# Two weight remainders of each state-space round on GpSimd, and the group's preparation done a round earlier

## The reference

```
h += 1/2 SwiGLU(RMSNorm(h))
u  = RMSNorm(h)
h += W_out( sum_b sigmoid(gate_b(u)) * P_b(mixer_b(u)) )   # linear attention, state space (SSD), chunk attention
h += 1/2 SwiGLU(RMSNorm(h));  out = RMSNorm(h)

SSD, for each of 8 groups (4 heads of 64, state 128), chunks of 64 tokens:
  x, B, C = silu(conv4(u @ w));  dt = softplus(..);  cum = cumsum(dt * a)
  y  = sum_s (C_t . B_s) * exp(cum_t - cum_s) * dt_s x_s        (s <= t, inside the chunk: "intra")
     + (C_t . state) * exp(cum_t)                                (from earlier chunks: "inter")
  state = exp(cum_last) * state + sum_s B_s (dt_s x_s exp(cum_last - cum_s))
  y  = RMSNorm_group((y + D x) * silu(z))
```

## Time and profile before

| | us |
|---|---|
| median of 3 runs | 1847.29 (1846.7 to 1848.17) |
| profiled execution | 1847.36 |
| its span, first to last instruction | 1845.5 |
| TensorE busy | 1806.9 |
| VectorE busy | 977.6 |
| ScalarE busy | 610.7 |
| GpSimd busy | 145.1 |

### The profile page before, as it was taken

How to read it: one execution, slowest core, us unless ns; L and a number is a source line. 1 busy time by engine, 2 the same in 40 slices (tenths; PEclk the granted TensorE clock), 3 DMA queues, 4 the chain that set the end, 5 groups by cost and what they waited for, 6 DMA issues and landing times.

```text
span 1845.5 us, 26225 instructions
## 1 busy us (share of the span) xinstructions
PE 1806.9 (98%) x9852; PEld 1508.4 (82%) x9852; DVE 977.6 (53%) x1376; ACT 610.7 (33%) x942; POOL 145.1 (8%) x116
## 2 busy tenths in 40 slices
PE   7999999999999999999999999999999999999997
PEld 5888888878888888788988888887888888888885
DVE  6444443379888888732444445545334544444333
ACT  4323222233333344332233334443222422323221
POOL 4111100031111111100000000000000011111000
PEclk9999999999999999999999999999999999999998
DMA  4323223322222222132222222222222322223331
GB/s 154 103 93 100 93 101 103 110 84 70 73 74 69 68 68 68 58 103 91 92 69 82 90 87 82 84 78 89 95 99 91 103 92 92 101 92 101 103 105 66
DMA packets 47352, 164.91 MB, mean 89 GB/s; under 512 B 5520, under 2 KB 6672, under 8 KB 47296
## 3 DMA queue, kind: packets, MB, share of 16 engines
q1 hardware_dynamic: 43584, 158.10, 26.1%
q10 hardware_dynamic: 3712, 6.03, 1.0%
HBM read 162.01 MB, written 2.10 MB: 89 GB/s over the span
## 4 chain that ended last, share of the span: by engine, by line
PE 70%; issue 21%; DVE 6%; POOL 1%; ACT 1%; DMA 0%; DVEq 0%; POOLq 0%; ACTq 0%; SPq 0%
PE G L534 33%; PE G L576 12%; PE I L534 9%; PE G L550 7%; DVE WL L1443 2%; DVE CV L1626 1%; PE I L896 1%; POOL hid L456 1%; PE I L930 1%; PE I L906 1%; PE I L704 1%; PE I L712 1%; PE G L761 1%; DVE UL L1459 1%; DVE un L1581 1%
## 5 line engine op out<-in xcount | busy, mean ns | idle before, releaser
L1443 DVE TENSOR_TENSOR WL<-RAW,WH 128x1024 fp32r<-128x1024 f32 x297 | 387.9, 1309 | 298.2 <-ACT WH L1025 290.2
L1025 ACT CAST WH<-RAW 128x1024 fp32r<-128x1024 f32 x297 | 309.6, 1048 | 230.9 <-PE I L534 126.2
L534 PE MATMUL G<-UH,WH 128*128 128x512 f32 x696 | 172.8, 390 | 0.0
L534 PE MATMUL G<-UH,WL 128*128 128x512 f32 x696 | 171.9, 389 | 0.0
L534 PE MATMUL G<-UL,WH 128*128 128x512 f32 x696 | 171.9, 389 | 0.0
L534 PEld LDWEIGHTS G<-UH,WH 128*128 128x128 f32 x696 | 130.6, 188 | 28.0 <-issue 1.0
L534 PEld LDWEIGHTS G<-UH,WL 128*128 128x128 f32 x696 | 130.6, 188 | 27.1
L534 PEld LDWEIGHTS G<-UL,WH 128*128 128x128 f32 x696 | 130.6, 188 | 27.1
L534 PE MATMUL G<-NH,WH 128*128 128x512 f32 x448 | 113.2, 395 | 1.4 <-ACT SC L1098 1.4
L534 PE MATMUL G<-NL,WH 128*128 128x512 f32 x448 | 110.7, 389 | 0.0
L534 PE MATMUL G<-NH,WL 128*128 128x512 f32 x448 | 110.6, 389 | 0.0
(11 more groups left out here) (299 smaller groups left out, 2477.5 us busy)
## 6 DMA issues: line engine op xcount, KB each, us to landing
RAW<-in_slabs SPq DMA_DIRECT2D x297, 512.0 KB, 3.3
h<-in_x SPq DMA_DIRECT2D x4, 512.0 KB, 6.8
bias<-in_rel ACTq DMA_DIRECT2D x16, 128.0 KB, 3.0
out_y<-h ACTq DMA_DIRECT2D x8, 256.0 KB, 2.2
bias<-in_rel ACTq DMA_DIRECT2D x16, 112.0 KB, 2.6
cst<-in_cst SPq DMA_DIRECT2D x1, 168.0 KB, 3.6
ut<-in_wgk SPq DMA_DIRECT2D x3, 32.0 KB, 8.8
```

The lines of the kernel that those rows point to most:

```text
L534: ins = mm(dst, W[:, n.slot, (k - k0) * P:(k - k0 + 1) * P], R[:, k, :], start=begin and which == 0 and k == k0, stop=end and which == 2 a ...
L1025: nc.scalar.copy(WH[:, n.slot, :], RAW[:, n.slot, :]).then_inc(split_hi, 1)
L1443: V.tensor_tensor(WL[:, n.slot, :], RAW[:, n.slot, :], WH[:, n.slot, :].bitcast(F32), ALU.subtract).then_inc(split_lo, 1)
```

## The change

GpSimd takes over the remainders of slabs n+5 and n+6 of each looped round (`lo`), and VectorE waits for them ahead of n+7 so that the count split_lo stays in order. GpSimd makes MSL of the next group in this round, and VectorE makes MSH (`da_hi`) behind the silu of CT, both from SC and no longer from gsc. D times x is made by ScalarE while it copies x (four pieces, one for each head), XTE and XDT are read from PSUM, XTE first, and TensorE's updates wait for both. The squares are scaled by 1/16 and come ahead of the tanh of t=3; the variance is an addition on GpSimd; ScalarE scales two of the four tiles of Y and VectorE the others. `ssm_y` comes after the silu of t=2. In `ssm_intra` the two halves of a tile of tokens alternate with each matmul, where before four matmuls of one half followed each other. In ScalarE's round the rounding of slab n+3 comes between the copy of B and the exponential.

The diff is cut: left out are the new constant four_eps (4 x EPS) and its memset, and the places where `turn_back` gets its new argument.

```diff
@@ -113,18 +113,18 @@
 "conv_begun": 4, "conv_tanh": 4, "x_copied": 1, "b_copied": 1, "decay_exp": 1, "z_tanh": 2,
-"ssm_squares": 4, "ssm_hi": 2,
+"ssm_squares": 4, "ssm_scaled_act": 2, "ssm_hi": 2,
 "gla_exp": 1, "gla_kt_copied": 1, "gla_r_tanh": 2, "gla_squares": 4, "gla_hi": 2,
...
 "conv_const": 1, "group_const": 1, "group_norm": 1, "da_hi_masked": 1, "xdt_ready": 1, "xte_ready": 1, "cb_masked": 1,
-"m_ready": 1, "conv_done": 4, "ssm_chain": 13, "ssm_y": 4, "ssm_var": 1, "ssm_scaled": 4, "ssm_lo": 2,
+"m_ready": 1, "conv_done": 4, "ssm_chain": 13, "ssm_y": 4, "ssm_scaled": 2, "ssm_lo": 2,
 "gla_t": 2, "gla_qh": 1, "gla_qt": 1, "gla_kh": 1, "gla_a_masked": 1, "gla_chain": 7, "gla_var": 1,
...
     },
-    "gpsimd": {"da_lo_masked": 1, "xd_ready": 1, "ssm_rstd": 1, "gla_rstd": 1},
+    "gpsimd": {"da_lo_masked": 1, "ssm_var": 1, "ssm_rstd": 1, "gla_rstd": 1},
     "tensor": {
@@ -352,6 +353,8 @@
+causal_all = causal[:].unsqueeze(1).unsqueeze(1).to_broadcast([P, TT, HPG, CH])
+
 def over_tiles(ap):
@@ -428,20 +432,24 @@
-        pool.wait_ge(sems["group_const"], after("group_const", g))
         pool.wait_ge(sems["intra_done"], last("intra_done", g - 1))
-        inc(nc.gpsimd.tensor_tensor(MSL[:].rearrange("p (q t) -> p q t", t=CH),
-                                    bc(gsc[:, 28:32, :].rearrange("p j r -> p (j r)"), CH),
-                                    causal[:].unsqueeze(1).to_broadcast([P, TT * HPG, CH]), ALU.mult),
+        inc(nc.gpsimd.tensor_tensor(MSL[:].rearrange("p (j r t) -> p j r t", j=TT, t=CH),
+                                    bc(SC[:, 28:32, bass.ds(HPG * g, HPG)], CH), causal_all, ALU.mult),
             "da_lo_masked")
+    def lo(n):
+
+        pool.wait_ge(split_hi, n.value + 1)
+        pool.wait_ge(split_lo, n.value)
+        nc.gpsimd.tensor_tensor(WL[:, n.slot, :], RAW[:, n.slot, :], WH[:, n.slot, :].bitcast(F32),
+                                ALU.subtract).then_inc(split_lo, 1)
+
     def ssm(g):
-        pool.wait_ge(sems["xte_ready"], after("xte_ready", g))
-        pool.wait_ge(sems["group_norm"], after("group_norm", g))
-        d = ggrp[:, 2:6].unsqueeze(1).unsqueeze(3).to_broadcast([P, TT, HPG, CH])
-        x4 = XD[:].rearrange("p j (r c) -> p j r c", r=HPG)
-        inc(nc.gpsimd.tensor_tensor(x4, x4, d, ALU.mult), "xd_ready")
+        pool.wait_ge(sems["ssm_squares"], last("ssm_squares", g))
+        pool.wait_ge(sems["ssm_scaled"], last("ssm_scaled", g - 1))
+        pool.wait_ge(sems["ssm_scaled_act"], last("ssm_scaled_act", g - 1))
+        inc(nc.gpsimd.tensor_tensor(var4[:], ss4[:], four_eps[:], ALU.add), "ssm_var")
         pool.wait_ge(sems["ssm_var"], after("ssm_var", g))
@@ -496,9 +504,17 @@
     da_split()
-    with pool.Fori(0, NG) as i:
-        da_lo(i)
+    pool.wait_ge(dt_pool, DA_SPLIT)
+    da_lo(0)
+    with pool.Fori(0, NG - 1) as i:
+        n = At(N_SSM + 6, i, 6)
+        pool.wait_ge(sems["conv_begun"], after("conv_begun", i + 1, 2))
+        lo(n + 5)
+        da_lo(i + 1)
+        pool.wait_ge(sems["ssm_y"], last("ssm_y", i))
+        lo(n + 6)
         ssm(i)
+    ssm(NG - 1)
@@ -685,6 +701,7 @@
         pe.wait_ge(sems["xte_ready"], after("xte_ready", g))
+        pe.wait_ge(sems["xdt_ready"], after("xdt_ready", g))
         pe.wait_ge(sems["x_copied"], after("x_copied", g))
@@ -698,11 +715,11 @@
-        for c in range(NCH):
-            j, s = c // 2, half(c)
+        for j in range(TT):
             for rr in range(HPG):
-                ins = mm(I01[s, j * 256 + rr * CH:j * 256 + (rr + 1) * CH], M[s, j, rr, :],
-                         XDT[s, j, rr * CH:(rr + 1) * CH], start=True, stop=True)
+                for s in (half(0), half(1)):
+                    ins = mm(I01[s, j * 256 + rr * CH:j * 256 + (rr + 1) * CH], M[s, j, rr, :],
+                             XDT[s, j, rr * CH:(rr + 1) * CH], start=True, stop=True)
         inc(ins, "intra_done")
@@ -715,7 +732,8 @@
-        pe.wait_ge(sems[ready], last(ready, g))
+        for name in ready:
+            pe.wait_ge(sems[name], last(name, g))
         for f in range(2):
@@ -795,7 +813,7 @@
             0: lambda: ssm_turn(i), 1: lambda: ssm_cb_u(i), 3: lambda: (ssm_inter(i), ssm_intra()),
-            7: lambda: turn_back(Y, I01, "ssm_scaled", i, "ssm_turned")})
+            7: lambda: turn_back(Y, I01, ("ssm_scaled", "ssm_scaled_act"), i, "ssm_turned")})
@@ -1097,7 +1115,7 @@
-    def conv_begin(p, t, n, wn):
+    def conv_begin(p, t, n, wn, weights=True):
@@ -1108,7 +1126,7 @@
               bias=gconv[:, 5 * t + 4:5 * t + 5], scale=gconv[:, 5 * t + 3:5 * t + 4]), "conv_begun")
-        if not raw:
+        if weights and not raw:
             hi(n + 3)
@@ -1126,25 +1144,38 @@
-    def ssm_copy_exp(g):
+    def ssm_copy_exp(g, n=None):
         act.wait_ge(sems["xb_turned"], after("xb_turned", g))
         act.wait_ge(sems["ssm_y"], last("ssm_y", g - 1))
-        inc(nc.scalar.copy(XD[:].rearrange("p j c -> p (j c)"), I01[:]), "x_copied")
+        act.wait_ge(sems["group_norm"], after("group_norm", g))
+        for rr in range(HPG):
+            ins = A(XD[:, :, rr * CH:(rr + 1) * CH],
+                    I01[:].rearrange("p (j c) -> p j c", j=TT)[:, :, rr * CH:(rr + 1) * CH], ACT.Copy,
+                    scale=ggrp[:, 2 + rr:3 + rr])
+        inc(ins, "x_copied")
         act.wait_ge(sems["u_done"], last("u_done", g - 1))
         inc(nc.scalar.copy(BK[:].rearrange("p j c -> p (j c)"), I2[:]), "b_copied")
+        if n is not None:
+            hi(n)
         act.wait_ge(sems["seg_done"], after("seg_done", g))
...
-    def squares(src, dump, dst, name, g):
+    def squares(src, dump, dst, name, g, scale=1.0):
...
             act.wait_ge(sems[name], after(name, g, j - 1))
-            inc(A(dump[:], src(j), ACT.Square, accum_out=dst[:, j:j + 1]), name)
+            inc(A(dump[:], src(j), ACT.Square, scale=scale, accum_out=dst[:, j:j + 1]), name)
...
         act.wait_ge(sems["ssm_chain"], last("ssm_chain", g))
-        squares(lambda j: Y[:, j, :], ssm_dump, ss4, "ssm_squares", g)
+        squares(lambda j: Y[:, j, :], ssm_dump, ss4, "ssm_squares", g, 1.0 / 16)
+
+    def ssm_scale(g):
+
+        act.wait_ge(sems["ssm_rstd"], last("ssm_rstd", g))
+        for j in range(TT // 2):
+            inc(A(Y[:, j, :], Y[:, j, :], ACT.Copy, scale=rstd4[:, j:j + 1]), "ssm_scaled_act")
@@ -1202,11 +1233,13 @@
         for t in range(4):
-            conv_begin(p, t, n + t, wn + t)
+            conv_begin(p, t, n + t, wn + t, t > 0)
             if t == 0:
-                ssm_copy_exp(inner)
+                ssm_copy_exp(inner, n + 3)
+            if t == 3:
+                ssm_squares(inner)
             conv_tanh(p, t, wn + t)
-        ssm_squares(inner)
+        ssm_scale(inner)
         z_tanh(p, n + 4, wn + 4)
@@ -1223,6 +1256,7 @@
     ssm_squares(g)
+    ssm_scale(g)
     evict_hi(I01, SH, 2 * g, ssm_norm_cols, "ssm_turned", g, "ssm_hi")
@@ -1604,10 +1638,12 @@
         dve.wait_ge(sems["group_const"], after("group_const", g))
-        dve.wait_ge(sems["intra_done"], last("intra_done", g - 1))
-        da = gsc[:, 24:28, :].rearrange("p j r -> p (j r)")
-        inc(V.tensor_tensor(MSH[:].rearrange("p (q t) -> p q t", t=CH), bc(da, CH),
-                            causal[:].unsqueeze(1).to_broadcast([P, TT * HPG, CH]), ALU.mult), "da_hi_masked")
+
+    def da_hi(g):
+
+        dve.wait_ge(sems["seg_done"], after("seg_done", g - 1))
+        inc(V.tensor_tensor(MSH[:].rearrange("p (j r t) -> p j r t", j=TT, t=CH),
+                            bc(SC[:, 24:28, bass.ds(HPG * g, HPG)], CH), causal_all, ALU.mult), "da_hi_masked")
@@ -1661,11 +1697,11 @@
         dve.wait_ge(sems["x_copied"], after("x_copied", g))
+        inc(V.tensor_tensor(XTE[:].rearrange("p j (r c) -> p (j r) c", c=CH), heads(I01[:]), rows(2),
+                            ALU.mult), "xte_ready")
         dve.wait_ge(sems["intra_done"], last("intra_done", g - 1))
-        inc(V.tensor_tensor(XDT[:].rearrange("p j (r c) -> p (j r) c", c=CH), heads(XD[:].rearrange("p j c -> p (j c)")), rows(1),
+        inc(V.tensor_tensor(XDT[:].rearrange("p j (r c) -> p (j r) c", c=CH), heads(I01[:]), rows(1),
                             ALU.mult), "xdt_ready")
-        inc(V.tensor_tensor(XTE[:].rearrange("p j (r c) -> p (j r) c", c=CH), heads(XD[:].rearrange("p j c -> p (j c)")), rows(2),
-                            ALU.mult), "xte_ready")
@@ -1707,17 +1743,15 @@
         dve.wait_ge(sems["ssm_y"], after("ssm_y", g, 1))
-        dve.wait_ge(sems["xd_ready"], after("xd_ready", g))
+        dve.wait_ge(sems["x_copied"], after("x_copied", g))
         inc(V.tensor_tensor(yf, yf, XD[:].rearrange("p j c -> p (j c)"), ALU.add), "ssm_y")
...
-        dve.wait_ge(sems["ssm_squares"], last("ssm_squares", g))
-        inc(V.tensor_scalar(var4[:], ss4[:], 1.0 / 256, 4 * EPS, ALU.mult, ALU.add), "ssm_var")
         dve.wait_ge(sems["ssm_rstd"], last("ssm_rstd", g))
-        for j in range(TT):
+        for j in range(TT // 2, TT):
```

(20 more changed lines are left out.)

## The result

The changed kernel takes 1855.47 us (median of 6 runs, 1854.75 to 1857.18) against 1847.18 for the kernel before (6 runs): a ratio of 1.0044, 95% interval 1.0034 to 1.0055. The forecast was 1837.1, so 18 us are missing, and the sign is wrong.

The account below looks back on a forecast made before the run. TensorE, busy 98% of the span, was taken as the bound. Terms -6.7 - 3.6 + 0.7 + 1.75 - 2.3 = -10.2 us took 1847.36 to 1837.1 us (bounds 1833.0 and 1840.8), range 1832.5 to 1843.2.

Parts of the forecast that it names:

- nothing else is touched: Opening paragraph: reason for reading TensorE's rows over the state-space rounds only; no term for matmuls elsewhere.
- D: Intra matmuls: alternation breaks the overlap of weight loads, 63 ns per instruction, slower at 1851.8 us; chance 0.05.
- Part 1: Looped rounds: TensorE's waits for MSL and XTE vanish, 1.12 us in each of six rounds, 6.7 us saved.
- about 43.5: Looped rounds: expected period in us between the first NH matmuls, six of them, as a sign of being right.
- Part 2: Intra matmuls: alternating quarters overlap, 0.52 us saved per group (bounds 0.4 and 0.65), 3.6 us over seven rounds.
- Rival A: Intra matmuls: the new order overlaps no more than the old, costing 8 x 0.52, so 1841.3 us; chance 0.08.
- Part 3: GpSimd's remainders beside VectorE's state chain: 2.4 us each, one chain step held, the chain just in time.
- the charge of 0.7: Inter matmuls: cost in us for the state chain ending late, 0.1 in each of seven rounds.
- Rival B: State chain really late: inter matmuls wait 0.8 us per round, 1842.0 us; chance 0.14.
- Part 4: Round's end: Y ready by C+27.6 to 28.6 (C: CT,BT matmuls' start), transposes ask at C+29.2, so no wait.
- rival C: Y transposes or z matmuls' bank: a new wait replaces the old two, losing the 6.7 us, 1843.8; chance 0.08.
- Part 5: Before the loop, first MSL delays VectorE's chain, +1.75 us (bounds 0.5 and 2.2); after the loop, tail -2.3 us.

Follow-up runs that it names:

- e1: Changed kernel with four_eps in the 16 unused bytes behind minus_half, so every tensor lies where it lay before: 1837.94 us, ratio 0.9948.
- e2: Kernel before with 16 unused bytes ahead of LR, moving every later tensor up by 32 bytes: 1864.36 us, ratio 1.0088.
- e4: e1 with the intra matmuls in the order of before: 1841.82 us, ratio 0.9969.
- e7: e1 with the remainders of slabs n+5 and n+6 back on VectorE and its wait for them gone: 1837.58 us, ratio 0.9948.
- e8: Kernel before with only the remainders of slabs n+5 and n+6 moved to GpSimd: 1847.59 us, ratio 1.0.

## Why the prediction was wrong, step by step

**The step that failed** is in the first paragraph of the prediction: "nothing else is touched". With it the sum put at nothing, without a reason, what the change does to all other matmuls; it took that every matmul outside the edited rounds keeps its duration. The diff had said otherwise, and I had even cut it: the constant `four_eps` seemed too small to print. It costs nothing to compute, but its declaration moves the tensors behind it. The price can be read from the counts and means of the groups. Of the 128x512 matmuls whose activations moved there are 1344 with NH or NL at L550, 480 more in the other such line, 1056 with HH or HL, 120 with SL and 336 with AH, AL, MH or ML: 3336 (56 more stand in other lines), at 6 ns (395 against 389) +20.0 us. Of 128x256 there are 1920. From start to start eleven times eight take 10.56 us in a round of before (550.04 to 560.60) and 10.42 in the changed one (554.49 to 564.91), 120 and 118.4 ns each: -3.1 us. Together +16.9; e1 against the changed kernel measured 17.5, e2 against the kernel before 16.5. None of my rivals held it. The 0.05 for "slower" was D and what I had not seen.

**Part 1, the two waits: right.** With the tensors at home a round of e1_home took 43.32 us (531.90 to 575.22, from its first XTE,BK row to the next), 1.74 less than before. That is 1.12 for the waits and 0.61 for the intra order. The two brackets of the earlier trace rows hold only 0.82 of the 1.12; the prediction was right to take the difference of the rounds, since the whole of it came back. The 43.69 of the changed kernel are these plus 0.37 from the slower matmuls. A reader who saw only 43.69 against my "about 43.5" would have taken the sum for right.

**Part 2, the intra order: right**, 2.08 instead of 2.69 (0.61; I took 0.52, from L684's pace), and 0.49 per group by e4. Rival A and the alternation's danger, D, are refuted by this row.
The Trainium skill ("TensorEngine Tiling (Array Packing)", Restrictions and Gotchas) says that different row tiles cannot use one PSUM bank at the same time. By that rule this part would have saved nothing. The trace disagrees as far as this order goes: alternating quarters into one bank became faster, 2.08 against 2.69. Whether two of them ever write in the same instant it does not tell.

**Part 3, GpSimd's remainders: right in mechanism, and the charge of 0.7 was not due.** VectorE's and GpSimd's rows of the changed kernel, the same round:

```profile
546.02 2.40 POOL L444 TENSOR_TENSOR WL<-RAW,WH 128x1024 fp32r<-128x1024 f32 x1 [27.55 <-ACT WH L1043]
546.53 2.17 DVE L1728 TENSOR_TENSOR ST<-SS,gsc 128x256 f32<-128x256 f32 x1
548.73 0.42 DVE L1732 TENSOR_TENSOR SS<-ST,I 128x256 f32<-128x256 f32 x1
```

The remainder takes the 2.4 I took; the step of the chain beside it is held for 2.17 instead of 0.42; the chain ends at 549.15, and the inter matmuls start at 549.56 without idle time. So the stall exists and is covered by 0.4 us (by 0.23 in e1_home, where the chain ends at 544.70 and the inter matmuls start at 544.93). Rival B did not occur. What I did not ask is whether moving the remainders gains anything: e7 and e8 say no. VectorE had the time.

**Part 4, the end of the round: right.** No idle time stands before the transposes of Y or the z matmuls; rival C did not occur.

**Part 5, start and tail: the start was mis-sized.** The MSL did hold VectorE's remainder, 2.92 instead of 1.21, and so TensorE: the wait grew from 1.43 to 3.14 in e1_home, the 1.75 that I charged. But I left out what the clock can do after such a wait. The next eight matmuls took 1.35 more than their 2.11: the term is +3.1, not +1.75, in this trace. The second price does not hang on the early MSL alone. The traced execution of e8_before_lo_on_gpsimd, which has no early MSL, waited 2.91 there and ran its eight in 3.78 (it took 1850.92, the longest of its 11), and e4 did not pay it. In the tail (timeline of TensorE, changed kernel; the earlier trace rows before) both waits of the earlier trace rows shrank, and a third grew that the prediction has not, for the copy of B ahead of C times B (0.33 before):

```profile
749.96 0.69 PE L700 MATMUL I<-CT,BT 128*64 128x64 f32 x16 [1.43 <-ACT BK L1157]
751.91 2.08 PE L707 MATMUL I<-XTE,BK 64*128 64x256 f32 x8 [1.27 <-issue]
...
777.03 1.06 PE L739 MATMUL I<-ident,Y 128*128 128x128 f32 x8 [0.58 <-ACT Y L1178]
```

From the first matmul of the merge to the last transposes it was 37.73 us before and 34.99 in e1_home (734.51 to 769.50): 2.7 saved, where I had 2.3.

**The sum of the mechanisms.** With the tensors at home the change brought -9.9 us (e1: 1837.94 against 1847.84), where I had -10.2. The mechanisms of the rounds were right, but that the two numbers meet is in part luck: the start was too small by 1.3, while the stall (0.7), the intra order (0.6 over seven rounds) and the tail (0.4) came out better than charged. The layout, worth nearly twice the sum, was left out.

## What to carry to other kernels

Before trusting "the rest stays as it is", compare the addresses of the large operands in both programs: a scrap of a constant in the middle of the declarations moves all that is declared behind it, and here that outweighed a correct redesign. After a change, compare the mean durations of forms that nobody touched before explaining anything else. New small constants go to the end of the allocation or into an unused gap. Where an added wait makes TensorE idle, as here for 3.14 us, count the slow matmuls behind it too.
